# The down projection of the first sixteen SwiGLU tiles as seven-product steps between the gate/up steps of a two-layer decoder trunk

## The reference, cut to what matters

```
h2 = rms_norm(x, g_ffn[l])
gu = h2 @ w_gu[l]
x  = x + (silu(gu[..., :D_FF]) * gu[..., D_FF:]) @ w_down[l]
```

## Time and profile before

| | us |
|---|---|
| median of 3 runs | 2004.79 |
| lowest, highest | 2004.62, 2006.62 |
| span of the profiled execution | 2003.4 |
| TensorE busy in the span | 1982.9 (99%) |
| VectorE busy | 1124.1 (56%) |
| ScalarE busy | 801.7 (40%) |

### The profile page before, as it was taken

How to read it: one execution, slowest core, us unless ns; L and a number is a source line. 1 busy time by engine, 2 the same in 40 slices (tenths; PEclk the granted TensorE clock), 3 DMA queues, 4 the chain that set the end, 5 groups by cost and what they waited for, 6 DMA issues and landing times. The chain is left out here.

```text
span 2003.4 us, 42908 instructions
## 1 busy us (share of the span) xinstructions
PE 1982.9 (99%) x17043; PEld 1862.2 (93%) x17043; DVE 1124.1 (56%) x1796; ACT 801.7 (40%) x1275; POOL 130.5 (7%) x215
## 2 busy tenths in 40 slices
PE   9999999999999999999999999999999999999999
PEld 8968978999999999999998698799899999999999
DVE  6475413346445888953374743143664568998433
ACT  4365522223224365532234754232332345555222
POOL 0001120011000000000000012200100000000000
PEclk9999999999999999999999999999999999999999
DMA  6317683245334223342343267813543342333422
GB/s 211 127 35 239 205 284 105 76 147 179 106 107 148 77 80 99 105 132 87 99 154 130 81 217 234 282 53 95 169 142 119 101 129 63 106 105 88 135 87 94
DMA packets 259556, 262.10 MB, mean 131 GB/s; under 512 B 13354, under 2 KB 224466, under 8 KB 258642
## 3 DMA queue, kind: packets, MB, share of 16 engines
q1 hardware_dynamic: 241074, 190.69, 30.5%
q0 software_dynamic: 18208, 69.22, 10.6%
q10 hardware_dynamic: 128, 0.15, 0.0%
HBM read 234.98 MB, written 25.03 MB: 130 GB/s over the span
## 5 line engine op out<-in xcount | busy, mean ns | idle before, releaser
L1734 DVE TENSOR_TENSOR WL<-RAW,WH 128x2048 fp32r<-128x2048 f32 (+2 forms) x112 | 235.9, 2107 | 190.1 <-ACT WH L1260 190.0
L1260 ACT ACTIVATE WH<-RAW 128x2048 fp32r<-128x2048 f32 (+2 forms) x120 | 212.2, 1769 | 90.2 <-PE PS L766 87.2
L766 PE MATMUL PS<-XH,WH 128*128 128x272 f32 x1152 | 243.0, 292 | 0.6
L766 PE MATMUL PS<-XL,WH 128*128 128x272 f32 x1152 | 237.9, 288 | 0.0
L766 PE MATMUL PS<-XH,WL 128*128 128x272 f32 x1152 | 237.7, 288 | 0.0
L766 PEld LDWEIGHTS PS<-XH,WH 128*128 128x128 f32 x1152 | 180.7, 188 | 7.8 <-issue 5.2
L766 PEld LDWEIGHTS PS<-XL,WH 128*128 128x128 f32 x1152 | 181.0, 188 | 0.0
L766 PEld LDWEIGHTS PS<-XH,WL 128*128 128x128 f32 x1152 | 180.3, 189 | 0.0
L746 PE MATMUL PS<-WH,XH 128*128 128x256 f32 x512 | 152.1, 297 | 0.0
L747 PE MATMUL PS<-WL,XH 128*128 128x256 f32 x512 | 144.4, 282 | 0.0
L748 PE MATMUL PS<-WH,XL 128*128 128x256 f32 x512 | 143.7, 281 | 0.0
(11 more groups left out here) (395 smaller groups left out, 4688.3 us busy)
## 6 DMA issues: line engine op xcount, KB each, us to landing
RAW<-in_w_in SPq DMA_DIRECT2D x106, 512.0 KB, 4.6
RAW<-in_w_gu SPq DMA_DIRECT2D x128, 256.0 KB, 3.8
PG<-in_cache_k SPq DMA_DIRECT2D x64, 256.0 KB, 3.2
PG<-in_cache_k POOLq DMA_DIRECT2D x64, 256.0 KB, 3.2
RAW<-in_w_gu SPq DMA_DIRECT2D x24, 512.0 KB, 4.5
RAW<-in_w_down SPq DMA_DIRECT2D x32, 384.0 KB, 3.5
PG<-in_cache_v SPq DMA_DIRECT2D x44, 256.0 KB, 3.6
PG<-in_cache_v POOLq DMA_DIRECT2D x44, 256.0 KB, 4.1
```

The lines of the kernel that those rows point to most:

```text
L766: last = pe.matmul(PS[:, 2 * pair + h, 0:HALF], w[:, i, c0:c0 + P], block[:, h * HALF:(h + 1) * HALF], start=first and i == 0 and a == 0, ...
L1260: act.activation(WH[:, slot, 0:n], RAW[:, slot, 0:n], ACT.Copy).then_inc(hi_ready, 1)
L1734: dve.tensor_tensor(WL[:, slot, 0:n], RAW[:, slot, 0:n], WH[:, slot, 0:n].bitcast(F32), ALU.subtract).then_inc(lo_ready, 1)
```

## The change

The 16 tiles 0 to 15 are cut in two chunks of eight. The down projection of a chunk is four seven-product steps of a new kind "d", one for each pair of output tiles: two of the chunk's neighbouring hidden tiles are the two halves of K, the two output tiles the two halves of the output. The four d steps of chunk 0 stand behind the gate/up step of tile 8, those of chunk 1 behind the step of tile 16 (`seven_steps`), so that a layer has 24 steps where it had 16. Tiles 16 to 21 go through a plain final stage "dn": 8 output tiles with 6 K blocks, 36 matmuls each, 288 in a layer.

The moving operand of a d step is seven quadrants made from each pair of tiles, high and low, in the buffer KQ (4 pairs). For an even tile `hidden_sums` makes one difference of 272 columns and `hidden_high`/`hidden_low` one quadrant of 272; for an odd tile `hidden_sums` makes three sums of 272, then `hidden_high` casts six quadrants (6 x 272) and `hidden_low` makes their six low parts. These stand last in each step on both engines. On ScalarE `t12_high` moves ahead of the copy behind product 5. The sigmoid and `gate_mul` become one Silu on ScalarE. The value of an odd tile lives in VB, of an even tile in EA. A d step's result is added by three VectorE operations of 544 columns (`part_added`) to x in XP, which GpSimd fetches from `x_parked` in four pieces, the first after product 6 of step 0, the others after product 6 of step 2; `residual` then adds the final tiles. All loops over steps and output tiles are written out. Buffers are laid out anew, and two of the four quadrant sums of the input (SF) reuse the space of the others.

The diff, cut to its core (a line of "..." where something is left out):

```diff
+NC = 6
+CHUNK = 8
+NQ = FT // CHUNK * CHUNK
+NF = FT - NQ
+CUT = [CHUNK * (c + 1) for c in range(NQ // CHUNK)]
+def seven_steps():
+    out = []
+    for f in range(NC, FT):
+        out.append(("g", f, 0))
+        if f in CUT:
+            out += [("d", CUT.index(f), i) for i in range(KT // 2)]
+    return out
...
# TensorE
+                def moving(q, k, low):
+                    if kind == "g":
+                        return (Q11, QS1, QS2, Q12, QS3, QS4, Q22)[q][low][:, k, :]
+                    return KQ[:, k, (0, 3, 4, 1, 5, 6, 2)[q], low, :]
...
+                pe.wait_ge(tile_free, lay * NT + T0["sv"] + 2 * s)
+                gate_read(s - 2)
+                if kind == "d" and i == 0:
+                    pe.wait_ge(hq_lo, lay * (2 * NPAIR) + CHUNK * (f + 1))
+                product(1, a_chunk("11"), a_bank, start=True).then_inc(prod, 1)
...
+            pe.wait_ge(x_lo, lay * NX + X0["fin"] + NF - 2)
+            for u in range(2):
+                split_ready(U0["dn"] + u)
+                gate_read(NSU - 2 + u)
                 for m in range(2):
+                    feature_tile(T0["dn"] + 2 * u + m, 2 * u + m, u, UC, m * P, range(NF), hidden, final=False, part=early)
+            pe.wait_ge(x_lo, lay * NX + X0["fin"] + NF)
...
+            for u in range(2, 4):
+                unit2(U0["dn"] + u, u % 2, T0["dn"] + 2 * u, range(NF), hidden)
# ScalarE
+            def hidden_high(f):
+                act.wait_ge(val_ready, lay * NVAL + value_at(f) + 1)
+                if f >= NQ:
+                    act.activation(HIDDEN_HI[f - NQ], value_of(f), ACT.Copy).then_inc(hi_val, 1)
+                    return
+                k = f // 2 % 4
+                if f % 2 == 0:
+                    act.activation(KQ[:, k, 0, 0, :], EA[:, 1, 0:HALF], ACT.Copy).then_inc(hq_hi, 1)
+                else:
+                    act.wait_ge(hs_ready, lay * (3 * NPAIR) + 3 * (f // 2) + 3)
+                    act.activation(KQ[:, k, 1:7, 0, :], VB[:], ACT.Copy).then_inc(hq_hi, 1)
...
+                copy(s, PS[:, b + 3, 0:HALF], b + 2, 2)
+                act.wait_ge(val_ready, lay * NVAL + V0N["gu"] + NC + s)
...
+                copy(s, EB[:, 1, 0:HALF], b + 1, 3)
+                if s < NSU - 1:
+                    t12_high(s + 1)
+                copy(s, EB[:, 1, HALF:N], b + 1, 5)
+                if late is not None:
+                    hidden_high(late)
...
# VectorE
+                dve.wait_ge(hs_ready, n + 1)
+                dve.tensor_tensor(VB[:, 3, :], odd[1], VB[:, 4, :], ALU.subtract).then_inc(hs_ready, 1)
+                dve.tensor_tensor(VB[:, 2, :], odd[1], even[1], ALU.add)
+                dve.wait_ge(hs_ready, n + 2)
+                dve.tensor_tensor(VB[:, 5, :], VB[:, 3, :], odd[0], ALU.subtract).then_inc(hs_ready, 1)
...
+            def part_added(s):
...
+                copies_made(s)
+                odd = halves(XP[:, 2 * i + 1, :])
+                dve.tensor_tensor(odd, odd, halves(EB[:, 1, :]), ALU.add).then_inc(val_ready, 1)
+                done(T0["sv"] + 2 * s + 1)
+                even = halves(XP[:, 2 * i, :])
+                dve.tensor_tensor(even, even, pair[2 * (s % 2)], ALU.add)
+                dve.wait_ge(val_ready, lay * NVAL + V0N["gu"] + NC + s + 1)
+                dve.tensor_tensor(odd, odd, pair[2 * (s % 2) + 1], ALU.subtract).then_inc(tile_free, 2)
...
+                if kind == "g":
+                    up_sum(s - 1)
+                    t34_low(s)
+                    gated_up(s - 1)
+                    if f not in CUT or f == NQ:
+                        late = f
...
+                    a_low(s + 1)
+                    w_sums(s + 1)
+                    t12_low(s + 1)
+                if late is not None:
+                    hidden_sums(late)
+                    hidden_low(late)
```

More of the change, by code:

```diff
@@ L1654, in _ @@
-            with act.Fori(0, KT // 2) as i:
-                for m in range(2):
-                    down(i, m)
+            quad_hi(3, QS2, SF[1][:])
+            a_high(0)
+            ahead("gp", 2, 0, 2)
+            silu(3)
+            hidden_high(3)
+            t12_high(0)
+            silu(4)
+            t34_high(0)
+            hidden_high(4)
+            a_high(1)
+            first_seven()
+            for s in range(1, NSU):
+                seven(s)
+            gate_high(NSU - 1)
@@ L2259, in _ @@
-            seven(NC + 1, 1)
-            with own.loop(FT // 2 - NC // 2 - 2, 0) as i:
-                for j in range(2):
-                    seven(2 * i + (NC + 2 + j), j)
-            seven(FT - 2, 0)
-            seven(FT - 1, 1)
-            up_sum(FT - 1, 1)
-            gate_mul(FT - 1, 1)
-            gated_up(FT - 1)
-            hidden_low(FT - 1)
-            def down(i, m):
-                k = 2 * i + m
-                split(4 * i + (U0["down"] + 2 * m + 1), 1, 11 * P)
-                split(4 * i + (U0["down"] + 2 * m + 2), 0, 8 * UC)
-                residual(k + T0["down"], m, k, 24 * lay + k + 8, lay * NX + k + (X0["down"] + 1),
-                         (2 * lay + 2) * KT + k, (xf_back, lay * 16 + 16))
+            gu(NC - 1, lambda: t12_low(1))
@@ L2277, in _ @@
+            hidden_sums(NC - 1)
+            hidden_low(NC - 1)
+            for s in range(1, NSU):
+                seven(s)
+            up_sum(NSU - 1)
+            gated_up(NSU - 1)
+            hidden_low(FT - 1)
             own.mark(dve.memset(EB[:, 1, :], 0.0))
-            hold(dve, x_lo, lay * NX + (X0["gu"] + FT))
+            dve.wait_ge(x_lo, lay * NX + (X0["fin"] + NF))
             dve.tensor_tensor(GD[:], IDENT.unsqueeze(1).to_broadcast([P, KT, P]),
@@ L2281, in _ @@
             own.hold()
-            with own.loop(KT // 2, 0) as i:
-                for m in range(2):
-                    down(i, m)
+            for i in range(2):
+                for j in range(2):
+                    ahead("dn", i, j, NF * UC if i + j < 2 else 8 * UC)
+                    for m in range(2):
+                        k = 4 * i + 2 * j + m
+                        residual(k + T0["dn"], 2 * j + m, k, 24 * lay + k + 8, lay * NX + k + (X0["dn"] + 1),
+                                 (2 * lay + 2) * KT + k)
             assert own.n == LAYER_MARKS, f"marks of a layer: {own.n}"
```

546 lines of the change are left out of this document (289 added, 257 removed).

## The result

The changed kernel takes 2036.58 us (median of 4 runs, 2034.70 to 2038.59), the kernel before 2004.70 (4 runs, 2003.89 to 2006.62): a ratio of 1.0159, 95% interval 1.0146 to 1.0171. The profiled execution of the changed kernel is the fastest of the four: 2034.7 us with a span of 2033.0, 29.6 more than before. I had forecast a median of 2038 and a span of 2036.9.

What follows compares the result with a forecast made beforehand. TensorE alone was taken to set the end. Per layer -11.6 + 8.2 + 8.3 + 2.4 + 0.2 + 5.8 = +13.3, plus 3.4 for the clock, +16.7; twice that on span 2003.4, median 1.4 above: 2038 us, range 2026 to 2052.

Steps and rivals of the forecast that it cites:

- What is removed: Down projection: 8 d steps and 288 final matmuls replace 1056 matmuls, 11.6 us saved per layer; d steps cost no wait.
- third unit: Final stage: its split stands behind both residuals, so TensorE waits 3.9 us per layer.
- The odd tile's chain: Odd gate/up steps: sums, six-quadrant cast and difference end at 14.6 us, 4.0 after the step's end, making TensorE wait.
- Product 3: Steps behind tiles 9, 11 and 13: ScalarE's copy behind product 1 comes at 4.0 instead of 3.02, 1.0 us wait.
- Even steps: Even-tile gate/up steps: copy behind product 5 at 8.96, product 7 due at 9.05; 0.2 us a layer taken.
- Final stage: Three waits per layer: second unit 0.3 to 0.4, third unit 3.9, last sum about 1.5 late; sum 5.8 us.
- The clock: Granted clock falls behind the two 4.1 us waits a layer, 1.7 us each, 3.4 a layer; likeliest case, chance 0.45.
- The rival with the clock up (2031): Whole kernel: same waits but no clock dips, no 3.4 us a layer, 2031 us; chance 0.25.
- The rival with falls behind all short waits: Clock also falls at about 5 waits of 1.7 us a layer, 8.5 more: 2048 to 2055; chance 0.12.
- Gain real: Rival: odd tile's chain lies hidden, 23.1 us saved, only the final stage's part paid: 1982 to 1993; chance 0.10.
- half of the waits: Rival: 24 us of waits instead of 50, about 2006, no change; chance 0.08.
- the deciding point: End of t12_low in an odd step: forecast 9.9 us; near 6 needed for the gain to be real.

Runs made afterwards that it cites:

- experiment 7: Changed kernel with the tile's work moved to the middle of each step and the paired final stage together: 1991.61 us, ratio 0.9935.
- experiment 4: Changed kernel with 28 useless matmuls ahead of the first d step's wait, 112 in the program: 2029.67 us, ratio 1.0127.
- experiment 5: Changed kernel with final-stage weight units 2 to 4 split between the two residuals of a pair, on both engines: 2036.94 us, ratio 1.0156.
- experiment 6: Changed kernel with splits between a pair's residuals, both sums first, and the second unit's split ahead of the scaled identity: 2027.69 us, ratio 1.0112.
- experiment 1: Changed kernel with ScalarE's copy behind product 5 put ahead of t12_high again: 2028.10 us, ratio 1.0115.
- experiment 3: Changed kernel with the tile's sums, cast and difference in the middle of each step, same work: 2001.36 us, ratio 0.9979.

## Why the prediction was right, point by point

- **What is removed: held.** 192 matmuls fewer, and d steps run without waits for weights or for parked x. With most waits out of the way (experiment 7) the kernel is faster than before. From the first product of layer 1 to that of layer 2 it needs 978.3 us where the kernel before needed 984.8, 6.5 less, with 3.1 us of waits still in it; with their restarts (counted below) they cost about 4.7, so the gain is some 11.2 a layer against 11.6 forecast.
- **How a wait is counted.** My waits were differences of dates; the trace's bracket counts from the modelled end of the last matmul. TensorE's timeline of the changed kernel around one of them:

```profile
1722.56 0.29 PE L1210 MATMUL PS<-QS4H,CH 128*128 128x272 f32 x1
1724.29 0.39 PE L1210 MATMUL PS<-Q22H,T34H 128*128 128x272 f32 x1 [1.43 <-ACT EB L1628]
1724.52 0.30 PE L1210 MATMUL PS<-Q22L,T34H 128*128 128x272 f32 x1
```

  A matmul lasts 0.29 here and the next starts 0.125 behind it when nothing is waited for. From 1722.56 to 1724.29 are 1.73 us, so the wait costs 1.73 - 0.125 = 1.60, which is 0.17 more than the bracket says, and the next matmul comes 0.23 behind, 0.1 more again. So a wait costs 0.27 more than its bracket. The 0.1 I had left out for all waits but the long ones. With the 0.17, the waits compare as follows, forecast and then measured: first d step 4.1 and 3.89 + 0.17 = 4.06; product 3 behind tiles 9, 11, 13: 1.0 and 0.81; product 7 there: 1.7 and 1.60; tile 5, both: 2.4 and 2.20; second unit 0.3 to 0.4 and 0.40; third unit 3.9 and 3.79.
- **The odd tile's chain: held to 0.1 us.** Three sums (0.43 each, forecast 0.44), cast 1.56 (1.57), difference 1.86 (1.86), all from sizes that the trace of before did not have. The straight lines through the sizes of the earlier trace rows, drawn on to 272 and 1632 columns, carried the whole forecast.
- **Product 3: 0.2 too long** each, the term of the sum that was most off among the short ones (0.6 a layer). I had each instruction follow the last at full duration with a hand-over; the rows overlap by some 0.08 us in a row, more often than I had allowed.
- **Even steps: 0.2 forecast, none measured.** The copy behind product 5 came just in time, as its 0.09 us of room said.
- **Final stage: the mechanism right, 1.5 too much.** I had the last sum late by 1.5 at the boundary on top of 3.9 for the third unit. No such wait is in the changed kernel. It was not wrong that VectorE's chain sets the end: in experiments 4 and 5, with the clock up in the final stage, the wait is there (0.62, 2.08). It is covered by the 1.5 us that the dip takes from TensorE, as the prediction said for the dip (no further price) but not for the wait itself. Counting one of the two was right: I counted the late sum, and the trace shows the fall. That both are 1.5 us is chance.
- **The clock: held, the likeliest case, with the price 0.2 too high.** Six long waits, six falls. I had priced one by the clock, 1.7 us, and it costs 1.5 in time: at 1000.70 in the changed kernel six matmuls take 1.36 us at half speed, where they take 0.75 at full speed, so that half the clock is not half the pace. The rival with the clock up (2031) is what experiment 4 comes near to, at 2029.7. The rival with falls behind all short waits is out for the profiled execution: 18 waits of 0.2 to 1.45 us, none with a fall. The other three executions show a mean granted clock of 0.992 and not 0.994, about 4 us of clock more in 2035 us (an estimate, as the figures are rounded), and are 1.8 to 3.9 us slower; where their further falls stood isn't on record.
- **The sum per layer, as measured:** -11.6 (kept as forecast) + 21.7 for waits (8.1 + 7.2 + 2.2 + 4.2) + 12 x 0.1 behind them + 3 x 1.5 = 4.5 for the clock, together +15.8; the trace has +15.9. (With the 11.2 of experiment 7 in place of 11.6 it is +16.2, so the books close to some 0.4.) The forecast's +16.7 was near because the waits, 1.7 too high in all (23.4 against 21.7), and a boundary wait of 1.5 that isn't there stood against 1.1 more for the clock (three falls of 1.5 for my two of 1.7) and 1.2 behind the waits, which I had left out. So the total is nearer than its terms deserve, and that part is luck.
- **Gain real, and half of the waits: out.** `t12_low` ended at 9.9 us in the odd step (735.0 - 725.1), the number that I had named as the deciding point.

## What to carry to other kernels

Before work is put last in a step, add up the in-order chain behind its last input, hand-overs between engines included: three small sums, a cast and a difference that wait for each other cost 35 us more here at the step's end than in its middle, where other work fills the time in which one engine waits for the other. Where one engine's chain paces a stage, removing the wait that the trace shows moves it to the chain's end; only a shorter chain pays. And once waits on TensorE can't be avoided, short ones can be cheaper than one long one: each restart cost 0.27 us, a fall of the clock 1.5. No run here trades one for the other with their sum kept, so this is an estimate from those two figures.

## What the runs showed of the hardware

- **When the clock fell.** Read in stretches of 1 us, the nine profiles have 26 waits of TensorE of 3.6 to 4.4 us, and 25 of them brought the granted clock down to its lower level; the one at 995.80 in experiment 4 left it at 1.00. One of 2.08 us at the layer boundary lowered it too (experiment 5, 0.57 over 4 us), and so did, in all nine, the one of 1.88 us near the program's start, behind small transposes. In dense matmuls no wait of 1.45 us or less did, in the profiled executions. The Trainium skill (TensorE: Matmul & The Clock Gate, section "Why this matters for your kernels") puts the danger at gaps longer than this 2.08 us and that 1.88; the measurement decides, so its rule sorts the short and the 3.6 to 3.9 us waits of the changed kernel rightly and misses these two. What sets the exception of experiment 4 is open.
- **Sparse work can lose the clock behind still shorter waits.** In the attention stage, which no edit touches, every profile has a wait of 0.67 and one of 1.13 us close together in each layer. The clock fell there in two of 18 cases (experiment 5, layer 2, and experiment 6, layer 1), by 1.7 us of clock. The eight matmuls behind the second wait take 1.09 us in the changed kernel, and there in experiment 5, with a mean granted clock of 0.70 from 1145 to 1150:

```profile
1146.99 1.97 PE L897 MATMUL PS<-FIX,PR 128*128 128x128 f32 x8 [1.13 <-DVE PR L1893]
```

  So executions of one kernel differ by such falls, and a single profile can't show that a wait of some length never brings one.
- **What a fall costs isn't one figure.** It was 1.7 us of clock, 1.5 in time, six times in the changed kernel. But seven of the 25 falls behind long waits took 3.4 us of clock (both layers of experiments 1, 3 and 6, layer 2 of 5). In experiment 6, which leaves the steps as they are, the same wait of 3.89 us ahead of the same product in layer 1 is one of them. Behind the wait that is 2.30 x 0.50 + 2.00 x 0.50 + 2.00 x 0.17 = 2.5 us of clock, and the 48 matmuls take 8.51 us instead of 6.28, 2.2 more. The mean of 0.67 over the ten us from 740 says 3.3, so the clock was down for the last 0.8 / 0.5 = 1.6 us of the wait already (the wait ends at 741.71); in the changed kernel it fell only behind the wait (736 to 740: 1.00).

```profile
740.00:750.00 10.00, 8.29 (x48) 0.67 0.65 219
...
741.70:744.00 2.30, 2.29 (x10) 0.50 0.45 180
744.00:746.00 2.00, 2.00 (x11) 0.50 0.75 224
746.00:748.00 2.00, 2.00 (x15) 0.83 0.96 269
```

- **Filling a wait with useless matmuls paid** where the clock had fallen: 112 of them took 6.9 us off the kernel (experiment 4).
